# Two quarters of the memory's value projection moved within TensorE's order of a 2-block transformer kernel

## The chip, the cores and the metric

One core of a Trainium2 chip runs the whole program. The metric is the device time of one execution in microseconds (us); lower is better. The kernel before has a median of 904.1 us over 3 runs.

## The reference, cut to what matters

All tensors are float32, 256 tokens of width 1024. A first block (a pooling mixer, latent attention and two gated feed-forward layers) is followed by a second one; the change lies in the second:

```python
z = rms_norm_2(x, mix_norm_g) @ w_in            # q, k/v of three branches, gates, gmlp, conv
y_nsa  = nsa_mixer(...)                          # compressed, selected and window attention, 8 heads of 64
y_gmlp = gmlp_mixer(...)
y_conv = conformer_conv_mixer(...)               # 31 taps, layer norm, silu
x = x + concat(rms(y_nsa), rms(y_gmlp), rms(y_conv)) @ w_out
# cross attention to a memory of 256 rows
m = rms_norm_2(mem, g_m)
k, v = m @ wk, m @ wv                            # v: 256 x 1024, depends on mem and wv alone
x = x + softmax(q k^T / 16) v @ wo
x = x + conv_ffn(x, ...)
```

Since k and v depend on the memory alone, their products can be placed anywhere ahead of the cross attention.

## The kernel before, in words

A float32 product is made of three faster ones: each operand is split in a high and a low part (`three`, lines 1812 to 1814: high x high, high x low, low x high). Weights come in blocks of 128 x 2048 through three rotating slots: SyncE loads the raw block, ScalarE writes the high part (L576), VectorE the low part (L1067), TensorE uses both and signals `block_used`. SyncE loads a block when the splits of the block three before it are done; ScalarE's high part waits for `block_used` of that block.

Every engine has a program of its own, written out by hand; they meet only in semaphores. In the mixing stage TensorE's order weaves four things together:

- the projections of `z` from `xh`/`xl`;
- window and selected attention in six batches (`BATCHES`, numbered 0 to 5). For batch b: `nsa_scores(b)` (mask L2306, scores L2309, needs ScalarE's exponentials of the batch before, which read the same banks), `nsa_turn(b, g)` for both groups (four transposes into bank 6, L2319, needs bank 6 read by ScalarE's last copy), and `nsa_pv(b, g)` (value products of 64 columns, L2332, needs that copy, L889);
- the compressed branch: hidden layer (64 products of 30 columns, L2382), its second layer (L2399, L2401), scores (16 matmuls of 30 columns, L2420, signals `sc_mm`), transposes of its probabilities (L2439) and `nsa_comp(t)` (512 columns, L2445);
- the memory's values, four blocks `mem5` to `mem8` of 8 x 256 weights each. `tokens_half(name, b, t, ...)` makes one half of such a block, 128 tokens by 256 columns, in 8 steps k of three matmuls: 24 matmuls of 256 columns. `mem7` and `mem8` write bank 7, half t=0 its first 256 columns and t=1 its last. ScalarE copies the bank out when both halves are done (`mem_block`, L626, signals `mem_out`).

Around the change, TensorE's order (lines 2405 to 2459) is: scores 4; turn (3,0); the gmlp's mixing (L2411); turn (3,1); pv (3,0); scores of the compressed branch (L2420); pv (3,1); scores 5; turn (4,0); transposes of the convolution's output (L2431); mem7 t=1; turn (4,1); pv (4,0); L2439; wait for `mem_out` 8; mem8 t=0; pv (4,1); turn (5,0); comp(0); turn (5,1); pv (5,0); comp(1); pv (5,1); then the wait of lines 2456 and 2457 for the normalised outputs (`comp_in`, `y_scaled`); `turn(yn, ...)` (L1829); mem8 t=1; wait for the split of the turned outputs; the row blocks of `w_out`.

What feeds it. VectorE, in order: the weight split of wout2 (L1067), after `sc_mm` the softmax of the compressed branch (L1595 to L1597), the maximum of batch 5 (L1443), the rest of the softmax (L1600 to L1606), the statistics and the layer norm of the convolution (L1610 to L1623, signals `cvln_done`), after ScalarE's hyperbolic tangent the convolution's output (L1626), comp_add(0) (L1481), the scaling of the outputs (L1633, signals `y_scaled`), comp_add(1) (L1481, signals `comp_in`). ScalarE, in order: copy (4,0), exponentials of batch 5 for group 0 (L881), squares (L946), copy of mem7 (L626), copy (4,1), exponentials, copy for the compressed branch (L964), the tangent (L966, waits for `cvln_done`), copy (5,0) (L889), squares of the convolution's output (L946), copy (5,1), high part of wout3. GpSimd turns the sums of squares into the factors that L1633 uses.

Of the kernel before, what the change touches and what calls it, by code (L numbers as in the profile page):

```python
# [25 lines left out]
KD = D // P  # L26
# [205 lines left out]
def build(nc, w, consts, bands, columns_in, positions_in, out):  # L232
# [17 lines left out]
    with ExitStack() as ctx:  # L250
        def sb(name, shape, dt=F32):
            return ctx.enter_context(nc.sbuf_tensor(name, shape, dt))
# [11 lines left out]
        mh = sb("mh", [P, KD, SEQ], F32R)  # L264
        ml = sb("ml", [P, KD, SEQ], F32R)
# [203 lines left out]
        def _(sp):  # L469
            def load(n):  # L470

                _, _, parts = blocks[n]
                if n >= 3:
                    sp.wait_ge(hi_done, n - 2)
                    sp.wait_ge(lo_done, n - 2)
                for v, (ks, cs_), src in parts:
                    sp.dma_start(v(raw[n % 3])[:, ks, cs_], src).then_inc(raw_full[n % 3], 32 // len(parts))
# [1331 lines left out]
        def _(pe):  # L1809
            def three(outp, a_hi, a_lo, b_hi, b_lo, start, stop, **kw):  # L1810

                pe.matmul(outp, a_hi, b_hi, start=start, stop=False, **kw)  # L1812
                pe.matmul(outp, a_hi, b_lo, start=False, stop=False, **kw)  # L1813
                return pe.matmul(outp, a_lo, b_hi, start=False, stop=stop, **kw)  # L1814

            def weights(name, k, c):

                n = at[name]
                pe.wait_ge(lo_done, n + 1)
                return k_view(wh[n % 3], k, c), k_view(wl[n % 3], k, c)  # L1820
# [460 lines left out]
                if f == 1:  # L2281
                    ins.then_inc(block_used, 1)

            def tokens_half(name, b, t, a_hi, a_lo):

                h_, l_ = weights(name, KD, 2 * P)
                for k in range(KD):
                    ins = three(bank[b][:, t * 2 * P:(t + 1) * 2 * P], a_hi[:, k, t * P:(t + 1) * P],
                                a_lo[:, k, t * P:(t + 1) * P], h_[:, k, :], l_[:, k, :], k == 0, k == KD - 1)
                if t == 1:  # L2290
                    ins.then_inc(block_used, 1)

            mem_block(5)

            tokens_half("mem6", 6, 0, mh, ml)
            norm(4, 16)
            tokens_half("mem6", 6, 1, mh, ml)

            def nsa_scores(b):
# [13 lines left out]
            def nsa_turn(b, g):  # L2313
                n = BATCHES[b][3]
                pe.wait_ge(n_exp, HEADS_DONE[b] + (g + 1) * n)
                if 2 * b + g > 0:
                    pe.wait_ge(n_out, 2 * b + g)
                for i in range(4):
                    ins = pe.transpose(bank[6][:, i * P:(i + 1) * P], s2[g][:, i * P:(i + 1) * P], ident)  # L2319
                ins.then_inc(n_t, 1)  # L2320

            def nsa_pv(b, g):
                t, br, j0, n = BATCHES[b]
                pe.wait_ge(n_out, 2 * b + g + 1)
                if t == 1:
                    pe.wait_ge(acc_out, br + 1)
                for j in range(n):
                    h = g * REP + j0 + j
                    for kt in range(t + 1):
                        i = j * (t + 1) + kt  # L2330
                        c = br * P + g * DH
                        ins = pe.matmul(bank[4 + br][:, h * DH:(h + 1) * DH], p2[g][:, i * P:(i + 1) * P],  # L2332
                                        vsw[:, kt, c:c + DH], start=(g, j0 + j, kt) == (0, 0, 0), stop=kt == t,
                                        skip_group_check=True)
                ins.then_inc(o_all, 1)
# [9 lines left out]
            pe.wait_ge(mem_out, 7)  # L2345
            columns("z_ksw", 6, xh, xl)
            tokens_half("z_vsw", 7, 0, xh, xl)
            pe.wait_ge(z_out, 4)
            pe.wait_ge(ws_out, 1)
# [63 lines left out]
            ins.then_inc(mix_mm, 1)  # L2413
            nsa_turn(3, 1)
            nsa_pv(3, 0)
            pe.wait_ge(cmp_out, 1)
            pe.wait_ge(vbd_set, 1)
            for t, j in ((t, j) for t in range(NT) for j in range(REP)):
# [12 lines left out]
                    ins = pe.transpose(bank[3][:, t * CW_ + c * P:t * CW_ + (c + 1) * P],  # L2431
                                       yc[:, c, t * P:(t + 1) * P], ident)
            ins.then_inc(ycs_t, 1)
            tokens_half("mem7", 7, 1, mh, ml)
            nsa_turn(4, 1)
            nsa_pv(4, 0)
            pe.wait_ge(pc_done, 1)
            for t in range(NT):
                pe.transpose(bank[2][0:120, t * P:(t + 1) * P], cm[3][:, t * 120:(t + 1) * 120], ident).then_inc(pc_t, 1)  # L2439
            pe.wait_ge(mem_out, 8)  # L2440
            tokens_half("mem8", 7, 0, mh, ml)
            nsa_pv(4, 1)

            def nsa_comp(t):
                pe.matmul(bank[2 + t][:, :], pct[0:120, t * P:(t + 1) * P], vbd[0:120, :], start=True, stop=True) \  # L2445
                  .then_inc(o_cmp, 1)
# [6 lines left out]
            pe.wait_ge(cvln_done, 1)  # L2453
            nsa_comp(1)
            nsa_pv(5, 1)
            pe.wait_ge(comp_in, NT)
            pe.wait_ge(y_scaled, 4)
            turn(yn, 0, range(4, KD))
# [114 lines left out]
```

## Time and profile before

| | |
|---|---|
| three runs | 903.55, 904.1, 904.75 us (median 904.1) |
| the profiled execution | 904.55 us, its span 902.7 us |
| TensorE (PE) busy | 887.9 us, 98% |
| VectorE (DVE) busy | 675.5 us, 75% |
| ScalarE (ACT) busy | 482.1 us, 53% |
| GpSimd (POOL) busy | 51.4 us, 6% |
| DMA | 153.49 MB, mean 170 GB/s |
| the mixing stage around the change | about 590 to 621 us of the span |

Times in rows are microseconds from the start of the span. A timeline merges equal instructions; the spans of merged matmuls overlap, so the distance between two starts tells what a group takes. The granted clock is TensorE's, as a share of its full speed. In this chip it has two levels, 1.2 and 2.4 GHz, so 0.50 is the lower one.

### The profile page before, as it was taken

Reading aid. Unit: us, or ns where it says so; the run is one execution under the profiler, and the core shown is the slowest. Engines: PE = TensorE matmul, PEld = TensorE weight load, DVE = VectorE, ACT = ScalarE, POOL = GpSimd, SP = SyncE. Lnnn points to the kernel's source line nnn. Section 1 sums busy time; section 2 is a strip of 40 time slices with the busy share of each in tenths; the row PEclk is TensorE's granted clock in tenths of the full one; section 3 lists DMA queues with packets and bytes.
Section 4 is the critical chain, followed back from the end, with each engine's and each line's share of the span. In section 5 each row is a group of like instructions: output and inputs, shape, how many; then the busy total and the mean of one; then the engine's idle time right before and its main releaser. Section 6 shows DMA issues by size and latency. Waiting matters only on the chain.

```text
span 902.7 us, 14534 instructions
## 1 busy us (share of the span) xinstructions
PE 887.9 (98%) x5284; PEld 785.1 (87%) x5284; DVE 675.5 (75%) x1016; ACT 482.1 (53%) x748; POOL 51.4 (6%) x90
## 2 busy tenths in 40 slices
PE   9999999999999999999999999999999999999996
PEld 7888888889988888888888999998898788888885
DVE  5896776777646688767777787986654799999997
ACT  6754444465565655444434735555543665556544
POOL 3300000020000000000000500001100000000000
PEclk9999999999999999999999999999999999999999
DMA  9986665452533858656645775212544566676631
GB/s 257 311 242 198 195 205 177 132 172 91 170 127 98 233 172 244 198 176 186 208 136 168 193 202 175 103 48 70 169 173 126 164 181 185 195 209 185 179 101 48
DMA packets 186599, 153.49 MB, mean 170 GB/s; under 512 B 6113, under 2 KB 171617, under 8 KB 186546
## 3 DMA queue, kind: packets, MB, share of 16 engines
q1 hardware_dynamic: 185794, 150.36, 55.3%
q0 software_dynamic: 752, 2.39, 1.0%
q8 instruction: 36, 0.59, 0.3%
q14 instruction: 17, 0.14, 0.0%
HBM read 151.17 MB, written 1.05 MB: 169 GB/s over the span
## 4 chain that ended last, share of the span: by engine, by line
PE 91%; ACT 4%; DVE 3%; issue 1%; DMA 1%; POOL 0%; SPq 0%; POOLq 0%; ACTq 0%
PE bank L1962 26%; PE bank L1968 13%; PE bank L1812 13%; PE bank L1814 13%; PE bank L1813 13%; PE bank L1928 2%; PE bank L1829 1%; PE bank L2309 1%; PE bank L1917 1%; DVE wl L1067 1%; ACT wh L576 1%; PE bank L2332 1%; PE bank L2508 1%; DMA x_tok<-in_x 1%; PE bank L2487 1%
## 5 line engine op out<-in xcount | busy, mean ns | idle before, releaser
L1962 PE MATMUL bank<-xhl,wh 128*128 128x512 f32 x1008 | 252.2, 392 | 0.0
L1962 PEld LDWEIGHTS bank<-xhl,wh 128*128 128x128 f32 x1008 | 185.0, 189 | 37.2
L1968 PEld LDWEIGHTS bank<-xhl,wl 128*128 128x128 f32 x1008 | 137.6, 190 | 9.7
L1968 PE MATMUL bank<-xhl,wl 128*128 128x256 f32 x1008 | 140.5, 282 | 0.0
L662 ACT ACTIVATE wh<-raw 128x2048 fp32r<-128x2048 f32 x57 | 109.0, 1912 | 51.1 <-PE bank L1968 48.3
L1206 DVE TENSOR_TENSOR wl<-raw,wh 128x2048 fp32r<-128x2048 f32 x57 | 130.1, 2282 | 0.2 <-ACT wh L662 0.2
L1067 DVE TENSOR_TENSOR wl<-raw,wh 128x2048 fp32r<-128x2048 f32 (+3 forms) x51 | 104.7, 2063 | 29.1 <-ACT wh L576 29.0
L1814 PE MATMUL bank<-dh,hl 128*128 128x512 f32 x264 | 103.4, 392 | 0.0
L1813 PE MATMUL bank<-dl,hh 128*128 128x512 f32 x264 | 103.1, 391 | 0.0
L1812 PE MATMUL bank<-dh,hh 128*128 128x512 f32 x264 | 103.0, 390 | 0.0
L576 ACT ACTIVATE wh<-raw 128x2048 fp32r<-128x2048 f32 (+3 forms) x52 | 90.0, 1742 | 22.3 <-DMA raw<-in_xattn_wq 5.7
L1198 DVE TENSOR_TENSOR dl<-draw,dh 128x1024 fp32r<-128x1024 f32 x66 | 80.3, 1219 | 3.4 <-ACT dh L638 3.4
L1155 DVE TENSOR_REDUCE gs<-bank 128x256 f32<-128x512 f32 x66 | 45.4, 687 | 48.1 <-PE bank L1968 47.9
L638 ACT ACTIVATE dh<-draw 128x1024 fp32r<-128x1024 f32 x66 | 69.4, 1055 | 14.9 <-PE bank L1814 14.8
L652 ACT ACTIVATE th<-gs 128x256 f32<-128x256 f32 x44 | 18.4, 419 | 89.7 <-DVE gs L1155 89.7
L1814 PEld LDWEIGHTS bank<-dh,hl 128*128 128x128 f32 x264 | 49.5, 188 | 10.3
L1812 PEld LDWEIGHTS bank<-dh,hh 128*128 128x128 f32 x264 | 49.9, 189 | 8.6 <-issue 0.4
L1813 PEld LDWEIGHTS bank<-dl,hh 128*128 128x128 f32 x264 | 49.6, 188 | 8.2
L677 ACT ACTIVATE hh<-pr 128x256 fp32r<-128x256 f32 x66 | 26.9, 408 | 45.1 <-DVE pr L1183 45.1
L1191 DVE TENSOR_TENSOR hl<-pr,hh 128x256 fp32r<-128x256 f32 x66 | 27.9, 423 | 30.7 <-ACT hh L677 30.7
L1713 POOL TENSOR_SCALAR st<-ss 128x1 f32<-128x1 f32 x18 | 9.5, 529 | 710.7 <-ACT junk L595 513.8
L1812 PE MATMUL bank<-wh,xhl 128*128 128x512 f32 (+2 forms) x138 | 48.1, 348 | 0.9 <-DVE wl L1067 0.9
(325 smaller groups left out, 1555.4 us busy)
## 6 DMA issues: line engine op xcount, KB each, us to landing
raw<-in_ffn_w_up SPq DMA_DIRECT2D x88, 512.0 KB, 6.0
draw<-in_ffn_w_down SPq DMA_DIRECT2D x66, 512.0 KB, 3.5
raw<-in_ffn_w_gate SPq DMA_DIRECT2D x44, 512.0 KB, 5.1
raw<-in_w_in SPq DMA_DIRECT2D x18, 512.0 KB, 5.4
raw<-in_mla_w_o SPq DMA_DIRECT2D x8, 512.0 KB, 3.7
raw<-in_xattn_wv SPq DMA_DIRECT2D x8, 512.0 KB, 4.7
raw<-in_w_out SPq DMA_DIRECT2D x8, 512.0 KB, 4.0
raw<-in_xattn_wq SPq DMA_DIRECT2D x8, 512.0 KB, 5.6
```

The source lines that it names most:

```text
L576: ins = act.activation(h, r, ACT.Copy)
L638: act.activation(dh[s][:, :], draw[s][:, :], ACT.Copy).then_inc(d_hi, 1)
L662: act.activation(wh[ns][:, :], raw[ns][:, :], ACT.Copy).then_inc(hi_done, 1)
L1067: ins = dve.tensor_tensor(l, r, h.bitcast(F32), ALU.subtract)
L1155: dve.tensor_reduce(gs[:, :], gate[:, :].rearrange("p (a s) -> p s a", a=2), AX.X, ALU.add) \
L1198: dve.tensor_tensor(dl[s][:, :], draw[s][:, :], dh[s][:, :].bitcast(F32), ALU.subtract) \
L1206: dve.tensor_tensor(wl[ns][:, :], raw[ns][:, :], wh[ns][:, :].bitcast(F32), ALU.subtract).then_inc(lo_done, 1)
L1812: pe.matmul(outp, a_hi, b_hi, start=start, stop=False, **kw)
L1813: pe.matmul(outp, a_hi, b_lo, start=False, stop=False, **kw)
L1814: return pe.matmul(outp, a_lo, b_hi, start=False, stop=stop, **kw)
L1962: pe.matmul(b[:, :].rearrange("p (a s) -> p a s", a=2), wh[ns][:, a:a + P], xhl[:, :, k, :], start=k == 0, stop=False, skip_group_check=True)
L1968: ins = pe.matmul(b[:, 0:SEQ], wl[ns][:, a:a + P], xh[:, k, :], start=False, stop=k == KD - 1, skip_group_check=True)
```

## The change

`tokens_half` gets a range of steps, and signals `block_used` only with the last step. The half t=1 of mem7 is cut in two: its first four steps (12 matmuls) stand between pv (3,0) and the scores of the compressed branch, the other four where the half was. The half t=0 of mem8 is cut in two: its first four steps stay, the other four come behind pv (5,1), in front of the wait for the normalised outputs. Nothing else is changed; no instruction on another engine and no DMA moves in its queue.

```diff
-            def tokens_half(name, b, t, a_hi, a_lo):
+            def tokens_half(name, b, t, a_hi, a_lo, ks=range(KD)):
 
                 h_, l_ = weights(name, KD, 2 * P)
-                for k in range(KD):
+                for k in ks:
                     ins = three(bank[b][:, t * 2 * P:(t + 1) * 2 * P], a_hi[:, k, t * P:(t + 1) * P],
                                 a_lo[:, k, t * P:(t + 1) * P], h_[:, k, :], l_[:, k, :], k == 0, k == KD - 1)
-                if t == 1:
+                if t == 1 and ks[-1] == KD - 1:
                     ins.then_inc(block_used, 1)
...
             nsa_turn(3, 1)
             nsa_pv(3, 0)
+            tokens_half("mem7", 7, 1, mh, ml, range(4))
             pe.wait_ge(cmp_out, 1)
             pe.wait_ge(vbd_set, 1)
...
             ins.then_inc(ycs_t, 1)
-            tokens_half("mem7", 7, 1, mh, ml)
+            tokens_half("mem7", 7, 1, mh, ml, range(4, KD))
             nsa_turn(4, 1)
...
             pe.wait_ge(mem_out, 8)
-            tokens_half("mem8", 7, 0, mh, ml)
+            tokens_half("mem8", 7, 0, mh, ml, range(4))
             nsa_pv(4, 1)
...
             nsa_pv(5, 1)
+            tokens_half("mem8", 7, 0, mh, ml, range(4, KD))
             pe.wait_ge(comp_in, NT)
             pe.wait_ge(y_scaled, 4)
             turn(yn, 0, range(4, KD))
```

## Rows read from the trace of the kernel before

**Rows 1.** The page's busy time of the engines: us, share of the span, instructions.

```profile
PE 887.9 (98%) x5284; PEld 785.1 (87%) x5284; DVE 675.5 (75%) x1016; ACT 482.1 (53%) x748; POOL 51.4 (6%) x90
```

**Rows 2.** TensorE's waits, whole span: us in total, times, longest.

```profile
PE bank L1829 <- DVE yn L1481: 0.8, 1, 0.8
```

**Rows 3.** TensorE's timeline, scores of batches 4 and 5: start, us, instruction.

```profile
591.35 0.36 PE L2306 MATMUL bank<-maskr,identr 128*128 128x256 f32 x1
...
593.39 0.60 PE L2319 MATMUL bank<-con,s 128*128 128x128 f32 x4
...
595.24 1.00 PE L2332 MATMUL bank<-vsw,gain 128*128 128x64 f32 x8
596.08 1.92 PE L2420 MATMUL bank<-kcm,qt 128*128 128x30 f32 x16
597.84 1.22 PE L2332 MATMUL bank<-vsw,gain 128*128 128x64 f32 x8
598.83 0.56 PE L2306 MATMUL bank<-maskr,identr 128*128 128x256 f32 x1
...
602.44 0.60 PE L2319 MATMUL bank<-con,s 128*128 128x128 f32 x4
```

**Rows 4.** Busy time by stretch: PE, PEld, DVE, ACT, POOL, clock, DMA share, GB/s.

```profile
594.90:598.50 3.60, 3.60 (x34) 3.60 (x34) 3.52 (x8) 2.36 (x9) 0.00 (x0) 1.00 0.03 7
598.50:602.10 3.60, 3.60 (x13) 3.06 (x13) 2.26 (x5) 0.46 (x2) 0.00 (x0) 0.53 0.41 131
571.30:575.20 3.90, 3.90 (x66) 3.86 (x65) 3.76 (x11) 2.73 (x7) 0.00 (x0) 1.00 0.72 269
```

**Rows 5.** TensorE's timeline: half of mem7, turn (5,1), pv (5,1), the turned outputs.

```profile
603.23 0.36 PE L1812 MATMUL bank<-wh,mh 128*128 128x256 f32 x1
603.43 0.28 PE L1813 MATMUL bank<-wl,mh 128*128 128x256 f32 x1
...
606.19 0.60 PE L2319 MATMUL bank<-con,s 128*128 128x128 f32 x4
...
612.78 0.63 PE L2319 MATMUL bank<-con,s 128*128 128x128 f32 x4
...
615.00 1.00 PE L2332 MATMUL bank<-vsw,gain 128*128 128x64 f32 x8
616.78 1.09 PE L1829 MATMUL bank<-con,yn 128*128 128x128 f32 x8 [0.78 <-DVE yn L1481]
```

**Rows 6.** VectorE's timeline, from the maximum of batch 5 to comp_add(1).

```profile
602.64 1.29 DVE L1443 TENSOR_REDUCE nst<-bank 128x2 f32<-128x512 f32 x2 [1.78 <-PE bank L2309]
...
610.00 0.69 DVE L1623 TENSOR_TENSOR e<-e,lng 128x512 f32<-128x512 f32 x1
611.38 0.69 DVE L1626 SCALAR_TENSOR_TENSOR yn<-e,e 128x512 f32<-128x512 f32 x1 [0.69 <-ACT e L966]
...
614.99 1.14 DVE L1633 TENSOR_SCALAR yn<-yn,lst 128x256 f32<-128x256 f32 x4 [1.39 <-POOL lst L1794]
616.04 0.68 DVE L1481 TENSOR_TENSOR yn<-bank,yn 128x512 f32<-128x512 f32 x1
```

**Rows 7.** ScalarE's timeline: exponential of batch 4, copy of mem7, tangent, copy (5,0), squares.

```profile
598.33 0.23 ACT L881 ACTIVATION_READ_ACCUMULATOR s<-bank,nst 128x1 f32 x1
...
606.39 0.60 ACT L626 ACTIVATE v_mem<-bank 128x512 f32<-128x512 f32 x1 [0.26 <-PE bank L1814]
...
610.72 0.63 ACT L966 ACTIVATE e<-e 128x512 f32<-128x512 f32 x1 [2.07 <-DVE e L1623]
612.04 0.60 ACT L889 ACTIVATE gain<-bank 128x512 f32<-128x512 f32 x1 [0.69 <-PE bank L2319]
612.53 0.41 ACT L946 ACTIVATE junk<-yn 128x256 f32<-128x256 f32 x1
```

**Rows 8.** The chain of waits, behind the second turn of the outputs: start, us, what.

```profile
628.47 1.81 ACT wh L576
630.31 2.30 DVE wl L1067
```

## The prediction

> **What bounds the kernel now.** I began with the page's busy table: TensorE (PE) is busy 98% of the span [rows 1], so the kernel's time is the sum of TensorE's products plus its few waits. The list of TensorE's waits came next: in the mixing stage, where the change lies, only one wait is long enough to be listed, 0.8 us in front of the first turn of the normalised outputs, ended by VectorE's L1481 [rows 2]. That is the wait which line 2456 spells out (comp_in), in front of which one quarter is put.
>
> Then I laid TensorE's order of time beside the granted clock. The scores of batch 4 (L2306, L2309) begin at 591.35 and the turn behind them at 593.39: 2.04 us. Those of batch 5 are the same products of the same size and take from 598.83 to 602.44: 3.61 us [rows 3]. The clock says why: it is 1.00 from 594.9 to 598.5, and 0.53 from 598.5 to 602.1 [rows 4]. So in that stretch the engine ran at its lower level of 1.2 GHz, not 2.4. What it did before the fall: a turn, the value products of batch 3, 16 matmuls of 30 columns (L2420, 1.76 us from start to start) and value products of 64 columns (L2332) [rows 3]. The value products right at the fall take 0.99 us from start to start, and those of 595.24, at full clock, 0.84 [rows 3]. The fall thus costs 3.61 - 2.04 + 0.15 = 1.72 us; 3.6 us x (1 - 0.53) = 1.69 by the clock row agrees. This is a loss which TensorE's 98% does not show.
>
> **Part 1: a quarter of mem7 moves in among the small products.** In the present order the half stands from 603.23 to 606.19, 2.96 us for 24 products: the first takes 0.20 us to the next start, each later one 0.12 [rows 5]. A quarter of 12 costs 0.20 + 11 x 0.12 = 1.52 us, and cutting a half in two repeats the slow first start: 2 x 1.52 - 2.96 = 0.08 us more TensorE work. The quarter comes in at 596.08, so L2420 starts at 597.60 and ends its pitch at 599.36, the value products at 600.20. No wait is added there: ScalarE's last exponential of the batch had started at 598.33 [rows 7]. VectorE, which waits for L2420's result, gets it about 1.5 us later, at 599.4; it was busy with a weight split until then, and behind its next steps it idled 1.78 us before L1443 [rows 6], which is the cover. If the cover were gone the cost would be up to 1.5 us.
>
> I take it that the twelve products of 256 columns keep the clock at 1.00. Then the scores run 600.20 to 602.24 against 602.44 now: **0.20 us earlier, although 1.52 us of work was put in front**. What is released is L1443, the maximum of batch 5, at the head of VectorE's chain to L1623 (602.64 to 610.00 + 0.69) [rows 6]: this chain and what hangs on it move by -0.20. For the clock I have no row with the quarter in place, so both ends stay: all 1.72 us gained, or none. I take all, since every row of dense products in this stage shows 1.00, and the fall follows the sparsest 3.6 us.
>
> **Part 2: TensorE behind it.** The turn at 602.24 and the convolution's transposes (0.79 us from 602.44 to 603.23 today), then only one quarter of mem7: it ends at 604.55 instead of 606.19. Here TensorE gets ahead of its suppliers and waits where it did not: for the copy of bank 7 (ScalarE at 606.39, 0.60 us [rows 7]; its queue moves by -0.2 and it no longer waits for mem7, hence -0.45) until about 606.55, some 0.5 us. The first quarter of mem8 ends at 608.07, and value products, turn and first compression product, the same three groups that take 2.22 us from 612.78 to 615.00 [rows 5], at 610.3. The next turn needs bank 6 read by ScalarE's copy of batch 5, which stands in ScalarE's queue behind the hyperbolic tangent of 610.72 [rows 7]. That starts at 610.52 now. Today the copy starts at 612.04, held back by TensorE's late turn; after the change it follows the tangent at its pitch of 0.49: 611.01. From copy start to turn start today is 612.78 - 612.04 = 0.74 [rows 5, 7], so the turn starts at 611.75, 1.03 us earlier than now, after 1.4 us of new idle time. These two waits swallow what the clock gave; they cost nothing more as long as part 3 holds.
>
> **Part 3: the other quarter of mem8 in front of the wait.** From the turn to the last value products is again 2.22 us, plus 0.85 for themselves: 611.75 + 3.07 = 614.82. The quarter then fills until 616.34. Against it stands the other way to the wait: the tangent releases L1626 at 611.38 - 0.20 = 611.18, done 0.69 later, so ScalarE's squares (L946) start at 611.9 instead of 612.53, -0.63 [rows 6, 7]. GpSimd, then VectorE's L1633 (614.99) and L1481 (616.04) follow at the same distance: L1481 starts at 615.41 [rows 6], and TensorE could go on at 616.15. So the quarter itself ends later, and the turn starts at 616.34 against 616.78: **-0.44 us**. Added up on TensorE: +0.16 for the two cuts, -1.72 for the clock, -0.78 for the wait that goes, +1.9 for the two new ones.
>
> **Part 4: downstream.** Rows after the turn move with it. VectorE's split is ready by about 619.8, before TensorE has ended the second half of mem8 at 620.15. The later wait for ScalarE's and VectorE's split of wout0 (628.47, 630.31 [rows 8]) hangs on TensorE's own turn and shifts equally. No DMA is moved; SyncE's loads wait for splits alone, and those follow the same chains. mem7's release comes 1.6 us sooner, yet ScalarE stands elsewhere in its queue, so I count nothing.
>
> **Sum.** The profiled execution took 904.55 us (span 902.7), 0.45 above the median of 904.1. 904.55 - 0.44 = 904.11; on the median 904.1 - 0.44, **903.7 us**. Bounds: +1.28 if the clock gives nothing, and -0.63 if the quarter were no longer than the other path. A measurement of this kernel can tell about 0.2% (1.8 us) from no change, so even a right mechanism stays within it.
>
> **Rivals.**
> 1. *The fall comes all the same (slower).* Twelve products may not be what holds the clock. For it: from 571.3 to 575.2 TensorE ran 64 products of 30 columns and the clock stayed 1.00 [rows 4], so small products alone do not explain the fall. Against it: those 64 are of another shape (64 columns of weights, 60 ns apart by 3.9 us / 66) and the clock fell where the products stood 110 ns apart (1.76 us / 16). Price: the scores end at 602.24 + 1.72 = 603.96 instead of 602.44; VectorE's chain moves by +1.52 and the turn by 1.72 - 0.44 = +1.28: 905.4. It decides from the point where L1443 starts later than 602.64 + 0.44. The Trainium skill (TensorE: Matmul & The Clock Gate, "HAM oscillation") lays a falling clock to idle gaps between bursts of matmuls; this trace disagrees, as the busy row is 3.60 of 3.60 us before the fall. By that rule filling a busy stretch would change nothing and this rival's time would come.
> 2. *The fall moves to the new gap.* With about 1.4 us idle before 611.75, and small products on both sides, the clock may drop near 613. Price again up to 1.72 us on the dense work behind: 905.4. For it: it is emptier than anything before 598.5. Against: both compression products of 512 columns lie in that stretch, and today 0.78 us of idle with eight transposes behind it [rows 5] passes at full clock.
> 3. *The executions before mostly had no fall.* Then 1.72 us is not there to gain and the change costs 1.28: 905.4. Against: such executions should show about 902.8, and the three runs start at 903.55.
> 4. *Nothing net.* The new waits are longer than I work out, by the 0.44: 904.1. For it: every step of parts 2 and 3 hangs on latencies of 0.05 to 0.1 us.
>
> **How the numbers follow.** Forecast 0.50; rival 1 0.15; rival 2 0.08; rival 3 0.07; rival 4 0.20. The forecast's own range is 903.0 to 904.3. The low end of the range is 902.9, with 0.1 below; the high end 905.2 reaches almost to rivals 1 to 3, whose prices are their upper bounds. All cases lie within 1.8 us of the median; what is left for a faster result of over 0.2% is a gain of the clock in places which this profile does not show, 0.05, and for slower a fall of the clock at both places, 0.06.
>
> **What would show it.** Right: the clock 1.00 from 594 to 604; scores of batch 5 in about 2.0 us, starting near 600.2; L1443 near 602.4; TensorE idle about 0.5 us before mem8 and 1.4 before the turn of batch 5; no wait, or under 0.1 us, before the turn of the outputs, near 616.3. Wrong: a clock of 0.5 in that stretch or near 613, or L1443 later than 603.1.

## The result: 0.24% slower, and the profile after

The changed kernel took 905.24 us in the median of 20 runs (903.61 to 908.8), the kernel before 903.7 in its 20 (903.15 to 907.03). The ratio is 1.0024, with an interval of 1.0016 to 1.0032: slower, where 903.7 was forecast as 0.44 below a median before of 904.1. That 904.1 came from three runs; that the kernel before has the forecast's 903.7 in its 20 is a coincidence. The profiled execution took 904.91 us (span 903.2).

The 20 runs fall into groups. Twelve took 903.61 to 905.31 us with a mean clock of 0.996 to 0.999; eight took 907.89 to 908.8 with 0.993. Of the kernel before one run of 20 lay at 907.03, the others at 905.81 or less.

TensorE's timeline of the profiled execution, which is one of the twelve (start, us, instruction; rows that answer to [rows 3] and [rows 5]):

```profile
591.82 0.36 PE L2306 MATMUL bank<-maskr,identr 128*128 128x256 f32 x1
...
593.86 0.60 PE L2319 MATMUL bank<-con,s 128*128 128x128 f32 x4
...
596.52 0.36 PE L1812 MATMUL bank<-wh,mh 128*128 128x256 f32 x1
...
598.04 1.86 PE L2421 MATMUL bank<-kcm,qt 128*128 128x30 f32 x16
599.74 1.08 PE L2332 MATMUL bank<-vsw,gain 128*128 128x64 f32 x8
600.63 0.36 PE L2306 MATMUL bank<-maskr,identr 128*128 128x256 f32 x1
...
602.67 0.60 PE L2319 MATMUL bank<-con,s 128*128 128x128 f32 x4
...
612.21 0.63 PE L2319 MATMUL bank<-con,s 128*128 128x128 f32 x4 [1.48 <-ACT gain L889]
...
614.43 1.00 PE L2332 MATMUL bank<-vsw,gain 128*128 128x64 f32 x8
616.76 1.04 PE L1829 MATMUL bank<-con,yn 128*128 128x128 f32 x8
```

The new quarter takes 598.04 - 596.52 = 1.52 us, and the scores of batch 5 take 2.04 where [rows 3] has 3.61. The turn of batch 5 waits 1.48 us for ScalarE's copy, and the turn of the outputs waits for nothing. The granted clock over the stretch that held the fall in [rows 4] (columns as there):

```profile
594.90:602.10 7.20, 7.20 (x61) 7.03 (x60) 6.23 (x13) 3.02 (x11) 0.00 (x0) 1.00 0.17 47
```

VectorE and ScalarE of the same execution, for [rows 6] and [rows 7]:

```profile
602.88 1.29 DVE L1443 TENSOR_REDUCE nst<-bank 128x2 f32<-128x512 f32 x2 [1.46 <-PE bank L2309]
...
610.23 0.69 DVE L1623 TENSOR_TENSOR e<-e,lng 128x512 f32<-128x512 f32 x1
611.61 0.69 DVE L1626 SCALAR_TENSOR_TENSOR yn<-e,e 128x512 f32<-128x512 f32 x1 [0.69 <-ACT e L966]
...
615.87 0.68 DVE L1481 TENSOR_TENSOR yn<-bank,yn 128x512 f32<-128x512 f32 x1
```

```profile
610.95 0.63 ACT L966 ACTIVATE e<-e 128x512 f32<-128x512 f32 x1 [2.43 <-DVE e L1623]
611.49 0.58 ACT L889 ACTIVATE gain<-bank 128x512 f32<-128x512 f32 x1
612.34 0.42 ACT L946 ACTIVATE junk<-yn 128x256 f32<-128x256 f32 x1 [0.28 <-DVE yn L1626]
```

Executions differ by up to 1.1 us in when they reach this stage, so I measure from the start of batch 4's scores to the turn of the outputs: 616.78 - 591.35 = 25.43 us in the execution of [rows 3, 5], 616.76 - 591.82 = 24.94 after the change. From here on "the stage" is this stretch. Against that one execution it is 0.49 us shorter, as forecast (0.44), and yet the kernel is slower. The experiments look for where that went.

### The profile page after: what moved, and what is told of

The parts are those of the page before. It is cut to its first block, busy times and chain, and to the rows that moved or that the text cites. A ratio compares the mean times of both kernels' runs of the same rounds, so it can differ in the third digit from the quotient of the medians.

```text
span 903.2 us, 14534 instructions
## 1 busy us (share of the span) xinstructions
PE 887.8 (98%) x5284; PEld 785.4 (87%) x5284; DVE 675.3 (75%) x1016; ACT 482.0 (53%) x748; POOL 51.7 (6%) x90
## 4 chain that ended last, share of the span: by engine, by line
PE 91%; DVE 4%; ACT 3%; issue 1%; POOL 0%; POOLq 0%; ACTq 0%; DVEq 0%
PE bank L1962 26%; PE bank L1968 13%; PE bank L1812 13%; PE bank L1814 13%; PE bank L1813 13%; PE bank L1928 2%; PE bank L1829 2%; PE bank L1917 1%; DVE wl L1067 1%; ACT wh L576 1%; PE bank L2309 1%; PE bank L2332 1%; PE bank L2510 1%; PE bank L2042 1%; PE bank L2489 1%
```

## The experiments

Two theories stood at the outset. **The gap theory**: the new idle 1.48 us lets TensorE's clock fall behind it in some executions. **The draw theory** (rival 3): the fall of [rows 4] is not a property of the kernel but a draw of each execution, and most have none; then there is nothing to win back and the quarter of mem7 only delays. The rival to both was that the falls of the clock lie elsewhere and come by chance.

**The changed kernel once more** (`both_again`, no edit).

> The changed kernel once more, unaltered. Of its 20 runs 8 took 907.9 to 908.8 us with a mean clock of 0.993, the others 903.6 to 905.3 with 0.996 to 0.999. The gap theory: TensorE's new idle time of 1.48 us between the first compression product and the turn of batch 5 (610.7 to 612.2) lets the clock fall there in some executions; about 4 in 10 runs again take over 907, and a profile of such a run shows the lower clock from about 612 on. The other-place theory: the falls lie elsewhere in the kernel and came by chance; then the share of such runs differs widely from 4 in 10, as in the kernel before (1 of 20).

12 runs: 905.09 us against 903.44 for the kernel before on the same chip, ratio 1.0021 (1.001 to 1.0032). Three of 12 lay at 907.75 to 907.94 with a clock of 0.993; the rest at 903.64 to 905.46. The group is there again, with the first draw in 11 of 32 runs. The profiled execution was not one of them: it took 903.81 us and had no fall of the clock before the kernel's last 5 us, so it does not tell where the others lose their time. Its stage took 616.21 - 591.28 = 24.93 us.

**The quarter of mem7 alone** (`mem7_alone`).

```diff
-            tokens_half("mem8", 7, 0, mh, ml, range(4))
+            tokens_half("mem8", 7, 0, mh, ml)
...
-            tokens_half("mem8", 7, 0, mh, ml, range(4, KD))
```

> Only the quarter of mem7 is moved; mem8's half is whole again in its old place, so TensorE has 1.5 us more to do ahead of the gap, which closes (1.48 to about 0). The gap theory: no or few runs over 907; median within 0.5 us of the kernel before, as the turn of the outputs comes at -0.2 (chain of VectorE) where the kernel before has a fall near 598 and at +1.5 where it has none. The theory that the cut of mem7 itself makes the slow runs: about 4 in 10 runs over 907, as with both.

904.46 us against 903.44, 1.0008 (0.9999 to 1.0017); highest run 905.23 of 11. None over 907, so the cut of mem7 does not make them. The turn of batch 5 waits for nothing, and the outputs' turn waits 1.17 us for VectorE. The stage took 617.02 - 592.23 = 24.79 us. The median missed its expectation (within 0.5 us of the kernel before): it is 904.46 - 903.44 = 1.02 us higher, and so is the stage against the execution without a fall that `before_again` shows below (24.79 - 23.77 = 1.02).

**The quarter of mem8 alone** (`mem8_alone`, and again as `mem8_alone_2`).

```diff
-            tokens_half("mem7", 7, 1, mh, ml, range(4))
...
-            tokens_half("mem7", 7, 1, mh, ml, range(4, KD))
+            tokens_half("mem7", 7, 1, mh, ml)
```

> Only the quarter of mem8 is moved in front of the wait; mem7's half is whole. The gap theory: TensorE reaches the turn of batch 5 about 1.4 us earlier than before, so a gap of 0.6 to 0.8 us opens, half of the one with both; runs over 907 are between 1 and 8 of 20, and the others take 0.3 to 0.5 us less than the kernel before. If the gap does not matter: no run over 907 beyond the 1 in 20 of the kernel before.

> mem8's quarter alone once more, for its interval: 903.13 against 903.44 in the first draw. Theory that part 3 is worth 0.5 us where no clock falls: median 0.3 to 0.6 below the kernel before, no run over 907. Rival: the gain was a draw, same median as before.

903.13 us against 903.44, 0.9996 (0.9988 to 1.0005); again 903.7 against 903.75, 0.9996 (0.9987 to 1.0005). No run of 23 over 904.88. TensorE's timeline of the first:

```profile
591.86 0.36 PE L2306 MATMUL bank<-maskr,identr 128*128 128x256 f32 x1
...
610.87 0.63 PE L2319 MATMUL bank<-con,s 128*128 128x128 f32 x4 [0.56 <-ACT gain L889]
...
615.41 1.04 PE L1829 MATMUL bank<-con,yn 128*128 128x128 f32 x8
```

The gap is 0.56 us and brings no fall in either profile; the stage takes 615.41 - 591.86 = 23.55 us, in the second profile 615.10 - 591.58 = 23.52. Two expectations were missed. Runs over 907 had been expected at this gap (1 to 8 of 20), and there is none. And the second draw was to lie 0.3 to 0.6 us below the kernel before and lies 0.05 below: a gain in the median is not shown.

**The kernel before once more** (`before_again`, no edit) is the control that the prediction lacked.

> The kernel before, unaltered, to see its mixing stage in an execution without a fall of the clock there; 7 of 10 runs of it take 903.0 to 903.7 us. The theory that the falls are a draw of each execution: no fall near 598, the scores of batch 5 take about 2.0 us instead of 3.61, L1443 starts about 1.7 us earlier than with the fall (near 601.0), and the turn of the outputs comes about 24.0 us behind the start of batch 4's scores instead of 25.43. If the fall near 598 belongs to the kernel: it is there again, 3.6 us and 25.4.

903.15 us. TensorE's timeline, its clock over the stretch of [rows 4], and VectorE:

```profile
591.10 0.36 PE L2306 MATMUL bank<-maskr,identr 128*128 128x256 f32 x1
...
597.59 1.08 PE L2332 MATMUL bank<-vsw,gain 128*128 128x64 f32 x8
598.48 0.36 PE L2306 MATMUL bank<-maskr,identr 128*128 128x256 f32 x1
...
600.53 0.60 PE L2319 MATMUL bank<-con,s 128*128 128x128 f32 x4
...
614.87 1.09 PE L1829 MATMUL bank<-con,yn 128*128 128x128 f32 x8 [0.78 <-DVE yn L1481]
```

```profile
594.90:602.10 7.20, 7.20 (x59) 6.94 (x58) 6.76 (x15) 3.42 (x11) 0.00 (x0) 1.00 0.25 90
```

```profile
600.73 1.29 DVE L1443 TENSOR_REDUCE nst<-bank 128x2 f32<-128x512 f32 x2 [0.22 <-PE bank L2309]
```

The draw theory holds. The same program, with no dense quarter among its small products, kept the clock at 1.00 this time; the scores take 600.53 - 598.48 = 2.05 us and the stage 614.87 - 591.10 = 23.77. The wait of 0.78 us in front of the outputs is there all the same. And VectorE idles 0.22 us before L1443, not 1.78: the cover on which part 1 of the prediction leaned was made by the fall itself. Three more profiles bear on it, since up to the scores of batch 5 `mem8_alone`, `mem8_alone_2` and `mem8_three` have the order of the kernel before: their scores take 2.06, 2.04 and 2.05 us. Of five profiled executions with that order one had the fall.

**Filling the gap** was tried in two ways. `gap_filled` puts mem8's second quarter inside it instead of in front of the wait:

```diff
             nsa_comp(0)
+            tokens_half("mem8", 7, 0, mh, ml, range(4, KD))
             nsa_turn(5, 1)
...
             nsa_pv(5, 1)
-            tokens_half("mem8", 7, 0, mh, ml, range(4, KD))
```

> Both halves are cut, but mem8's second quarter stands inside the gap, behind the first compression product and in front of the turn of batch 5, instead of in front of the wait. The gap theory: the idle 1.48 us is filled with 1.52 us of products, no run takes over 907, and the turn of the outputs comes at about the time of VectorE's path, a wait of 0.6 us or so before it being back; median 903.2 to 904.3. If the slow runs come from mem7's quarter among the small products: still about 4 in 10 runs over 907.

`idle_products` leaves the changed order and adds twelve products that nothing reads:

```diff
             nsa_comp(0)
+            h_, l_ = weights("mem8", KD, 2 * P)
+            for k in range(4):
+                three(bank[0][:, 0:2 * P], mh[:, k, 0:P], ml[:, k, 0:P], h_[:, k, :], l_[:, k, :], k == 0, k == 3)
             nsa_turn(5, 1)
```

> The changed kernel with 12 products more (the four first steps of mem8, written once more to a bank that is free), of no use, in the idle 1.48 us between the first compression product and the turn of batch 5. No other order is changed. The gap theory: the turn of batch 5 starts within 0.1 us of where it was, and no run takes over 907; median 904.0 to 905.2. If the 908 us runs have another cause (mem7's quarter, or mem8's in front of the wait): 3 to 4 runs in 10 over 907 again.

`gap_filled`: 905.01 us against 903.44, 1.0013 (1.0004 to 1.0022), highest of 11 runs 905.22. `idle_products`: 904.9 against 903.75, 1.0008 (1.0 to 1.0017), highest of 12 runs 905.09. No run of 23 over 907, where the changed kernel has 11 of 32; at equal chances so few would come by luck about once in 700 (my estimate, an exact test of these counts). The second is the cleaner proof: 616.30 - 591.36 = 24.94 us for the stage as with the change, the same order, more work, and the 908 us runs are gone. The median of `gap_filled` missed its expectation of 903.2 to 904.3: its stage takes 616.79 - 592.02 = 24.77 us, still 1.00 more than the kernel before without a fall. Filling cures the gap, not the quarter of mem7.

**Doubling the gap** (`gap_doubled`): all of mem8's half t=0 in front of the wait.

```diff
-            tokens_half("mem8", 7, 0, mh, ml, range(4))
             nsa_pv(4, 1)
...
-            tokens_half("mem8", 7, 0, mh, ml, range(4, KD))
+            tokens_half("mem8", 7, 0, mh, ml)
```

> mem7 is cut as in the change, but all of mem8's half t=0 stands in front of the wait, so the idle time ahead of the turn of batch 5 grows from 1.48 to about 3.0 us. The gap theory: nearly every execution has the lower clock from about 612 to 619, the median lies at 908 to 910 (907.9 for a run with such a fall, plus 1.5 for the quarter that now comes late), and the profile shows where. If the gap does not bring the fall: median 906.4 (904.9 + 1.5), and no more runs than 1 in 3 lie 3 us above the others.

908.43 us against 903.75 (9 runs; 1.0039, 1.0022 to 1.0055). Six of nine lay at 908.35 to 910.19 with a clock of 0.992 to 0.994, three at 905.85 to 905.96 with 0.998: two thirds instead of one third. "Nearly every execution" had been expected. With nine runs the larger share is not shown either: 6 of 9 against 11 of 32 would come by luck about once in eight (estimated in the same way). The profiled execution waited 2.40 us, not 3.0, since the copy of bank 7 also held TensorE for 0.67 us earlier; its lower clock lasted from 612.7 to 619.6:

```profile
612.70:616.10 3.40, 3.40 (x12) 2.37 (x12) 1.74 (x5) 2.31 (x3) 1.21 (x2) 0.51 0.00 0
616.10:619.60 3.50, 3.50 (x18) 3.50 (x18) 1.76 (x4) 0.00 (x0) 0.00 (x0) 0.50 0.00 0
```

That is the place and the length which the next profiles show for the changed kernel.

**Catching a 908 us run of the changed kernel** (`both_look_1` to `both_look_7`, no edit, one execution each).

> The changed kernel, one execution with its profile, in search of one of the third of its runs that take about 908 us. The gap theory: a run of 907.7 or more has the lower clock for about 6.8 us from 611 to 613 on, as the kernel with the doubled gap has from 612.8 on, and its turn of the outputs comes 3 to 3.5 us later than the 24.93 us behind the start of batch 4's scores; a run of 903.6 to 905.3 has not. If the fall of such a run lies elsewhere, the gap theory is wrong for the changed kernel.

> The changed kernel, one execution. At 907.7 us or more the gap theory wants the lower clock from 611 to 613 on for about 6.8 us; by the other-place theory a fall elsewhere. A run below: no fall in the mixing stage.

Six of the seven took 903.67 to 905.05 us, with no fall in the mixing stage. `both_look_5` took 907.98. TensorE's timeline:

```profile
591.41 0.36 PE L2306 MATMUL bank<-maskr,identr 128*128 128x256 f32 x1
...
611.81 0.63 PE L2319 MATMUL bank<-con,s 128*128 128x128 f32 x4 [1.47 <-ACT gain L889]
612.27 1.00 PE L2332 MATMUL bank<-vsw,gain 128*128 128x64 f32 x8
613.12 1.65 PE L2446 MATMUL bank<-vbd,kvc 120*128 120x512 f32 x2
614.55 1.81 PE L2332 MATMUL bank<-vsw,gain 128*128 128x64 f32 x8
616.12 0.56 PE L1812 MATMUL bank<-wh,mh 128*128 128x256 f32 x1
...
618.83 1.77 PE L1829 MATMUL bank<-con,yn 128*128 128x128 f32 x8
```

Its busy time and clock by stretch, and below them those of `both_look_7` (903.95 us):

```profile
608.00:612.30 4.30, 2.83 (x21) 2.03 (x20) 3.50 (x6) 1.60 (x5) 0.00 (x0) 1.00 0.00 0
612.30:615.70 3.40, 3.40 (x18) 2.55 (x17) 1.51 (x6) 2.94 (x6) 1.21 (x2) 0.67 0.02 5
615.70:619.10 3.40, 3.40 (x18) 3.40 (x18) 2.20 (x5) 0.00 (x0) 0.00 (x0) 0.50 0.00 0
```

```profile
608.00:612.30 4.30, 2.83 (x21) 2.03 (x20) 3.50 (x6) 1.62 (x4) 0.00 (x0) 1.00 0.00 0
612.30:615.70 3.40, 3.40 (x26) 2.92 (x26) 1.50 (x6) 2.80 (x5) 1.21 (x2) 1.00 0.02 5
615.70:619.10 3.40, 3.40 (x31) 3.40 (x30) 3.21 (x8) 1.57 (x4) 0.00 (x0) 1.00 0.00 0
```

Up to 612.3 the two executions are alike: TensorE is busy 2.83 of 4.30 us in both. Then one runs on at full clock and the other falls to 1.2 GHz at 613.49 and stays there to 620.31 (0.50 over the whole of that stretch), 6.8 us. The quarter in front of the wait, at 0.12 us a product elsewhere, takes 618.83 - 616.12 = 2.71 us instead of 1.52. The stage takes 618.83 - 591.41 = 27.42 us, 2.49 more than without the fall; 3 to 3.5 had been expected, and the second half of mem8 starts at the low clock too. That is where the rest is: from the turn of the outputs to the end of the span this execution takes 906.1 - 618.83 = 287.27 us, and `both_look_4` (904.91 us), 903.2 - 616.68 = 286.52. Together the fall costs 2.49 + 0.75 = 3.2 us, close to the distance between the medians of the eight and the twelve runs (908.18 - 904.92 = 3.26). None of the 11 timed runs over 907 was profiled; this one has their time and their clock, 0.993.

**A shorter piece** (`mem8_three`): mem7 as before, and three steps of mem8 instead of four in front of the wait (`range(5)` and `range(5, KD)`).

> mem7 as before; of mem8's half t=0 only three steps (9 matmuls, 1.1 us) stand in front of the wait, five stay. With four steps the turn of the outputs started 0.2 us behind the end of VectorE's L1481, at 23.5 us from the start of batch 4's scores (23.77 in the kernel before without a fall). If TensorE's last products were the bound there by that much, three steps give 23.3 to 23.45, the gap ahead of the turn of batch 5 shrinks from 0.56 to about 0.2 us, and the median is 0.3 to 0.5 us below the kernel before. Rival: the range of the single runs hides it, same median.

903.21 us against 903.76 (11 runs): 0.9989, 0.998 to 0.9998, the one version of the seven tried that beats the kernel before, by an interval that nearly touches 1, so luck is not excluded. The gap is 0.20 us, as expected. The stage did not shrink further (23.3 to 23.45 had been expected): 614.66 - 591.14 = 23.52 us. L1481 of VectorE ended at 613.92 + 0.68 = 614.60, 0.06 before the turn; now VectorE is the bound, not the products. From the start of batch 4's scores L1481 ends at 23.46 us, and in `mem8_alone` at 614.51 + 0.69 - 591.86 = 23.34, 0.12 us earlier. So the gain over `mem8_alone` is not shown by the traces, only the lack of anything over 903.7 in its runs.

## Why the prediction was wrong

**What bounds the kernel now.** Misread. The fall of the clock near 598 was taken for a part of the kernel, from one profiled execution. It was a draw. `before_again` shows an execution without it, and four of the five profiled executions with the old order up to there have none. The times agree, though they do not show it by themselves: in the 61 runs of the kernel before that stand beside the first two sets of experiments (35 and 26), 40 lie below 903.95 us, and the execution with the fall took 904.55. A few of its runs (4 of the 26, at 905.5 to 907.0) were long too, with a clock of 0.995 or 0.996; none of them was profiled. The 1.72 us of the sum was rightly sized for an execution with the fall (25.43 - 23.77 = 1.66 us; of the 0.15 put down to the value products only 0.10 was the clock, since they take 598.48 - 597.59 = 0.89 us at full clock, not 0.84). But there is nothing of it to gain in a typical execution. This is the step that failed: the term "-1.72 for the clock" in the sum of part 3, with "I take all" in part 1. It was priced as a gain against an execution that was no typical one; without it the same sum gives +1.28, and the stage measures +1.16.

**Part 1.** The mechanics came out: a quarter of 1.52 us, scores of 2.04 us, L1443 at 602.88 - 591.82 = 11.06 us from the start of batch 4's scores, where the text had put it at 602.44, 11.09 us from the start in [rows 3]. But from the typical execution it is 11.06 - (600.73 - 591.10) = 1.43 us later, not 0.20 earlier. The cover named for it, 1.78 us of idle time, is 0.22 without the fall.

**Part 2.** Right: the new wait before the turn of batch 5 measured 1.48 us (forecast 1.4), the copy follows the tangent at 611.49 - 610.95 = 0.54 (0.49), and mem8's first quarter stands 606.90 - 606.33 = 0.57 us behind the start of the transposes ahead of it, where 0.14 was the distance before: 0.43 us of wait (forecast 0.5). "They cost nothing more as long as part 3 holds" was wrong: the gap costs a fall of the clock in 12 of the 39 executions timed or looked at.

**Part 3.** Right in kind: the wait of 0.8 us is gone, and TensorE's own products are last, by 616.76 - 616.55 = 0.2 us. On its own it is worth 23.77 - 23.55 = 0.22 us, since the quarter ends later than VectorE would have let TensorE go. With mem7's quarter it is worth nothing (24.79 alone, 24.93 together).

**The rivals.** Rival 3, given 0.07, is what happened: price 1.28 by the text, 24.93 - 23.77 = 1.16 us by the traces. Its counter-argument was that executions without a fall "should show about 902.8". `before_again` shows why they need not: against the execution of [rows 3, 5] it reached the stage 0.25 us earlier, took 1.66 us less in it, and gave back 286.43 - 285.92 = 0.51 us behind it, where its clock fell at 708.5. That makes 903.15. Executions also reach the stage up to 1.1 us earlier or later than one another (591.10 to 592.23), which blurs a step of 1.7 us in three runs. Rival 2, given 0.08, happened beside it in a third of the executions, at 3.2 us where the text had 1.72: the lower clock lasted 6.8 us and not 3.4, over dense products. The upper end of 905.2 lay below the text's own price of these rivals, 905.4. By rival 3 alone the median would still have stayed inside: the twelve runs without the second fall have a median of 904.92 us, 1.22 above 903.7, close to the 1.16 of the stage. It is the eight at 908 us that move the median of all 20 up to 905.24. So both act at once, where the text had them as alternatives, and that the measured median stands so near the 905.4 of the rivals is partly luck. Rival 1 fell: the clock did not fall at 598 with the quarter in place, in none of the nine profiles of the changed kernel nor in the four of the variants that keep it. But as only one of the five profiles without the quarter has such a fall, this is no proof that the quarter prevents it.

**The rule on idle gaps** in the Trainium skill (TensorE: Matmul & The Clock Gate, "HAM oscillation"). The prediction used it for the stretch before 598, where the busy row contradicts it. For the gap at 610.7 to 612.2 the runs agree in kind: filled, 0 of 23 runs over 907; 1.48 us idle, 11 of 32; 2.4 us idle, 6 of 9 over 908. They do not agree in length: that section speaks of idle gaps longer than any of these, so by it none of them would have let the clock fall. The measurement decides.

**A second place of the same kind.** All 18 profiled executions, of whatever kernel, have an idle 2.24 us of TensorE further on, in front of the last feed-forward layer, where it waits for ScalarE. In the profiled execution after the change and in `both_again`:

```profile
709.14 3.25 PE L1829 MATMUL bank<-con,xn 128*128 128x128 f32 x16 [2.24 <-ACT xn L604]
708.62 2.06 PE L1829 MATMUL bank<-con,xn 128*128 128x128 f32 x16 [2.24 <-ACT xn L604]
```

In 10 of the 18 the clock falls near its end, between 0.3 us ahead of the first product behind it and 1.4 us after that product's start, and stays at 0.50 for 3.4 us (after the change from 709.8, in `before_again` from 708.5); in 8, `both_again` among them, it stays at 1.00. So this too is a draw of each execution at an idle stretch, with and without the change. It splits the changed kernel's executions below 907: the four profiled ones with it took 904.91 to 905.05 us, the four without it 903.67 to 904.25. From the turn of the outputs to the end it costs 0.5 to 1.0 us (286.4 to 286.8 against 285.9).

**What stays open.** The fall near 598 in the kernel before has no idle time in front of it, and what brings it is not shown. Of the median's 1.5 to 1.65 us the stage explains 1.16; the rest is in part the group at 908 us, which shifts the median of all runs. `gap_filled` has no such group and lies 1.57 above the kernel before with a stage 1.00 longer, but its interval (0.4 to 2.0 us) holds both. The fall near 709 came in 8 of the 13 profiles with mem7's quarter moved and in 2 of the 5 without. In `mem7_alone`, `gap_filled` and `idle_products` 9 of 11, 9 of 11 and 11 of 12 runs lie above 904.3, where the executions with it lie; of the kernel before it is 14 of the 61. Whether the later time of that stretch makes the fall likelier was not tried.

## What to carry to other kernels

One profiled execution is one draw: before a stall of a microsecond is counted as gain, look whether the runs of the same kernel are one group, and take a second profile. Work moved out of a stretch leaves a hole that must be priced for the clock and not just for its length. Where a piece is put in front of a wait, try the smallest that does it: three steps gave the same stage as four (23.52 us against 23.55) and left a hole of 0.20 us instead of 0.56.

## What was not expected of the hardware

An idle 1.48 us between small products was enough for the clock to fall behind it, in a third of the executions, for 6.8 us; behind 0.56 us and 0.20 us no run of 34 shows it. The fall came after the gap was over: in `both_look_5` TensorE worked again at 611.8 and the clock fell at 613.5, onto dense products, at a cost of 2.5 us in the stage and 3.2 us in all. Idle time that "costs nothing" by the chain of waits thus cost more, in such an execution, than the 0.78 us of wait that the change removed. And the same program does not lose its clock at the same places each time: at the 2.24 us of idle time that end near 709 (707.1 to 713.1) it fell in 10 of 18 executions.
